# Last layer of a three-layer model: GpSimd makes half of the low weight halves, the convolution sums in PSUM, heads read their queries in place

## The reference, cut to what matters

```
h    = rms_norm(stream)                       # 272 x 1024
proj = h @ w_in                               # conv input 2048, q 1024, k 256, v 256, q_idx 512, k_idx 64, w_idx 8, gates 2048
q, k, q_idx, k_idx = rope(...)                # rotary embedding: x*cos + rotate(x)*sin
a, gate = split(u_conv); c = a * sigmoid(gate)
c = sum over w in 0..30 of c[t-30+w] * dw_w[w]  + dw_b      # 31 taps per channel, 1024 channels
y_a = silu(layer_norm(c)) @ pw_out
score = sum over 8 index heads of w_idx * relu(q_idx . k_idx / 8)     # which keys a query may see
keep the 68 best keys of each query (meta keys always)
y_b = softmax(q . k, kept keys only) . v  @ w_o               # 8 heads of 128, 2 key groups
stream += (sigmoid(g_a) * y_a + sigmoid(g_b) * y_b) @ w_merge
stream += ffn(...); out = rms_norm(stream)
```

## Time and profile before

| what | us |
|---|---|
| median of the runs shown | 1202.35 |
| the profiled execution's own time | 1201.14 |
| its span | 1199.4 |
| TensorE busy | 1140.1 (95%) |
| VectorE busy | 793.7 (66%) |
| ScalarE busy | 573.8 (48%) |
| GpSimd busy | 81.7 (7%) |

### The profile page before, as it was taken

How to read it: one execution, slowest core, us unless ns; L and a number is a source line. 1 busy time by engine, 2 the same in 40 slices (tenths; PEclk the granted TensorE clock), 3 DMA queues, 4 the chain that set the end, 5 groups by cost and what they waited for, 6 DMA issues and landing times.

```text
span 1199.4 us, 22503 instructions
## 1 busy us (share of the span) xinstructions
PE 1140.1 (95%) x8981; PEld 1097.4 (91%) x8981; DVE 793.7 (66%) x1260; ACT 573.8 (48%) x818; POOL 81.7 (7%) x85
## 2 busy tenths in 40 slices
PE   5998899999999999999999899898899998999998
PEld 4997799999999999999999799798678998999997
DVE  4546755555557776565555598999878666778743
ACT  4546744444445565444444533342456536565541
POOL 0003020000113110200000000100100000000000
PEclk9999899999999999999999999999898998999999
DMA  7662064654775333565456364343221553545360
GB/s 222 208 195 71 4 208 141 198 178 159 228 254 175 127 122 106 181 206 181 152 191 204 110 172 154 120 138 112 69 71 55 164 169 109 198 151 191 124 211 36
DMA packets 190773, 181.74 MB, mean 152 GB/s; under 512 B 20911, under 2 KB 189116, under 8 KB 190699
## 3 DMA queue, kind: packets, MB, share of 16 engines
q1 hardware_dynamic: 190171, 178.61, 47.1%
q0 software_dynamic: 528, 2.10, 0.6%
HBM read 179.64 MB, written 1.05 MB: 151 GB/s over the span
## 4 chain that ended last, share of the span: by engine, by line
PE 84%; DVE 9%; ACT 4%; issue 1%; DMA 1%; POOL 1%; SPq 1%; DVEq 0%; ACTq 0%; POOLq 0%
PE ps L495 25%; PE ps L496 24%; PE ps L497 24%; DVE work L2088 3%; PE ps L651 2%; DVE w_lo L356 2%; PE ps L804 1%; ACT w_hi L347 1%; PE ps L908 1%; DMA conv_rows<-in_conv_dw_w 1%; POOL work L421 1%; PE ps L642 1%; PE ps L404 1%; PE ps L1687 1%; PE ps L1850 1%
## 5 line engine op out<-in xcount | busy, mean ns | idle before, releaser
L495 PE MATMUL ps<-u_hi,w_hi 128*128 128x256 f32 (+2 forms) x1864 | 534.3, 287 | 17.1 <-DVE u_lo L464 8.7
L496 PE MATMUL ps<-u_lo,w_hi 128*128 128x256 f32 (+2 forms) x1864 | 530.3, 284 | 0.0
L497 PE MATMUL ps<-u_hi,w_lo 128*128 128x256 f32 (+2 forms) x1864 | 529.6, 284 | 0.0
L356 DVE TENSOR_TENSOR w_lo<-raw,w_hi 128x2048 fp32r<-128x2048 f32 (+5 forms) x184 | 386.0, 2107 | 173.2 <-ACT w_hi L347 172.7
L495 PEld LDWEIGHTS ps<-u_hi,w_hi 128*128 128x128 f32 x1864 | 356.2, 191 | 20.1 <-issue 17.1
L497 PEld LDWEIGHTS ps<-u_hi,w_lo 128*128 128x128 f32 x1864 | 356.1, 191 | 0.0
L496 PEld LDWEIGHTS ps<-u_lo,w_hi 128*128 128x128 f32 x1864 | 355.7, 191 | 0.5
L347 ACT ACTIVATE w_hi<-raw 128x2048 fp32r<-128x2048 f32 (+5 forms) x184 | 319.6, 1755 | 29.7 <-PE ps L497 29.5
L496 PE MATMUL ps<-a_lo,w_hi 128*128 128x256 f32 x528 | 148.0, 280 | 0.0
L497 PE MATMUL ps<-a_hi,w_lo 128*128 128x256 f32 x528 | 147.6, 280 | 0.0
L495 PE MATMUL ps<-a_hi,w_hi 128*128 128x256 f32 x528 | 147.0, 278 | 0.1
(11 more groups left out here) (285 smaller groups left out, 1294.4 us busy)
## 6 DMA issues: line engine op xcount, KB each, us to landing
raw<-in_w_in SPq DMA_DIRECT2D x24, 1024.0 KB, 5.3
raw<-in_w_gate SPq DMA_DIRECT2D x22, 1024.0 KB, 5.4
raw<-in_w_up SPq DMA_DIRECT2D x22, 1024.0 KB, 5.4
raw<-in_ffn_up SPq DMA_DIRECT2D x22, 1024.0 KB, 5.1
raw<-in_w_down SPq DMA_DIRECT2D x16, 768.0 KB, 4.8
raw<-in_od_w_qkv SPq DMA_DIRECT2D x12, 1024.0 KB, 5.2
raw<-in_w_down SPq DMA_DIRECT2D x16, 640.0 KB, 4.6
raw<-in_ev_w_in SPq DMA_DIRECT2D x8, 1024.0 KB, 8.3
```

Of the source, the lines that this page charges most:

```text
L356: nc.vector.tensor_tensor(w_lo[t % RING][:, 0:n], raw[t % RAW][:, 0:n], w_hi[t % RING][:, 0:n].bitcast(F32), ALU.subtract).then_inc(lo_don ...
L495: nc.tensor.matmul(out_ap, a_h, b_h, start=start and n == 0, stop=False)
L496: nc.tensor.matmul(out_ap, a_h, b_l, start=False, stop=False)
L497: mm = nc.tensor.matmul(out_ap, a_l, b_h, start=False, stop=stop and n == len(pairs) - 1)
```

## The change

VectorE no longer makes the low halves of units 3, 5, 7, ... 21; GpSimd does, in four pieces of 128x512 each, with a semaphore of its own (`pool_lo_done`), for which TensorE and SyncE then wait. The convolution's sums of the first three pairs of tiles lie in PSUM banks 6 and 7 and are written to `work` with the last tap; those of the fourth pair stay in SBUF. Rope and index scores are moved to banks 4 and 5 alone. The steps of the convolution are dealt out anew: 30 in `ph_conv`, 14 in `ph_idx`, 18 in `ph_proj`, 1 and 12 as before, then 15 in one loop behind `ph_gate` (all that is left of the first three pairs), then the fourth pair's 30 between the attention heads. The index heads multiply the queries in place by two zero-padded copies of the keys (`ki_half`, made by ScalarE), the attention heads read `q_d` in place, and GpSimd's sixteen copies of queries go.

```
@@ -251,7 +251,7 @@
         k_d = sb("k_d", [P, KVH, T2], scope=s)
         v_d = sb("v_d", [P, 3, KVH * DH], scope=s)
         wi = sb("wi", [P, 3, IH], scope=s)
-        q_cur = sb("q_cur", [P, 2, T2], scope=s)
+        ki_half = sb("ki_half", [P, 2, T2], scope=s)
         pick = sb("pick", [P, 416], BF16, scope=s)
         top8 = sb("top8", [P, 2, 8], scope=s)
         need = sb("need", [P, 2], scope=s)
@@ -318,8 +318,11 @@
             count[(ph.u0 + n) % RAW] += 16 * d
             landed.append(count[(ph.u0 + n) % RAW])
 
+    pool_units = [ph_conv.u0 + n for n in range(3, 23, 2)]
+
     raw_landed = [sem(f"raw_landed{n}") for n in range(RAW)]
     hi_done, lo_done, unit_done = sem("hi_done"), sem("lo_done"), sem("unit_done")
+    pool_lo_done = sem("pool_lo_done")
     pair_read = [sem(f"pair_read{n}") for n in range(4)]
 
     def pairs_read(eng, ph):
@@ -346,11 +349,31 @@
         wait(nc.scalar, unit_done, turn * ph.body + (t - (RING - 1)))
         nc.scalar.activation(w_hi[t % RING][:, 0:n], raw[t % RAW][:, 0:n], ACT.Copy).then_inc(hi_done, 1)
 
+    def wait_lo(eng, u, first=0):
+
+        if isinstance(u, int):
+            if u in pool_units:
+                eng.wait_ge(pool_lo_done, pool_units.index(u) + 1)
+                return
+            first = u
+        wait(eng, lo_done, u + (1 - sum(t < first for t in pool_units)))
+
+    def split_lo_pool(t):
+
+        nc.gpsimd.wait_ge(hi_done, t + 1)
+        for piece in range(4):
+            cols = slice(piece * UNIT // 4, (piece + 1) * UNIT // 4)
+            a = nc.gpsimd.tensor_tensor(w_lo[t % RING][:, cols], raw[t % RAW][:, cols], w_hi[t % RING][:, cols].bitcast(F32),
+                                        ALU.subtract)
+        a.then_inc(pool_lo_done, 1)
+
     def split_lo(ph, i, k):
 
         if (u := split_unit(ph, i, k)) is None:
             return
         turn, t, n = u
+        if t in pool_units:
+            return
 
         nc.vector.wait_ge(hi_done, turn * ph.body + (t + 1))
         nc.vector.tensor_tensor(w_lo[t % RING][:, 0:n], raw[t % RAW][:, 0:n], w_hi[t % RING][:, 0:n].bitcast(F32),
@@ -512,7 +535,7 @@
     def begin_unit(ph, i, k):
         s = (ph.u0 + k) % RING
 
-        nc.tensor.wait_ge(lo_done, ph.unit(i, k) + 1)
+        wait_lo(nc.tensor, ph.unit(i, k), ph.u0)
         if k % ph.group == 0:
 
             wait(nc.tensor, pair_read[ph.pair(k)], ph.used_before(i, k))
@@ -1093,7 +1116,8 @@
 
     def begin_load(ph, i, k):
 
-        wait(nc.sync, lo_done, ph.unit(i, k) - (RAW - 1))
+        if not isinstance(i, int) or ph.unit(i, k) >= RAW:
+            wait_lo(nc.sync, ph.unit(i, k) - RAW, ph.u0)
         nc.sync.sem_inc(sem("slot_taken"), 1)
         s = (ph.u0 + k) % RAW
         return raw[s], raw_landed[s]
@@ -1263,24 +1287,11 @@
         fold_squares("final", T1)
 
         pairs_read(pool, ph_down1)
-        for n, t in enumerate((cin[:, :, 0:CONV_W - 1], stat4[:], q_cur[:])):
+        for n, t in enumerate((cin[:, :, 0:CONV_W - 1], stat4[:], ki_half[:])):
             nc.gpsimd.memset(t, 0.0).then_inc(sem("zeroed"), 1)
             pool.wait_ge(sem("zeroed"), 4 + n)
-        pool.wait_ge(sem("rope_done"), 8)
-        for n in range(IH):
-            e = n % 2
-            rows = slice(64 * e, 64 * e + 64)
-            wait(pool, sem("idx_pad"), n)
-            wait(pool, sem("idx_scored"), n - 1)
-            nc.gpsimd.tensor_copy(q_cur[rows, e, :], qi[rows, n // 2, :]).then_inc(sem("idx_pad"), 1)
-        pool.wait_ge(sem("idx_scored"), IH)
-        pool.wait_ge(sem("idx_pad"), IH)
-        pool.wait_ge(sem("rope_done"), 18)
-        for i, e in dsa.steps(pool):
-            n = dsa.head(i, e)
-            wait(pool, sem("at_scores"), n + (dsa.base - 1))
-            wait(pool, sem("pad_done"), n + dsa.base)
-            nc.gpsimd.tensor_copy(q_cur[:, e % 2, :], q_d[:, n, :]).then_inc(sem("pad_done"), 1)
+        for t in pool_units:
+            split_lo_pool(t)
         fold_squares("ffn2", NF)
         fold_squares("final2", T1)
 
@@ -1510,12 +1521,19 @@
                 nc.scalar.activation(v_d[0:META, 0, :], ps[0:META, 2 * p, UC:2 * UC], ACT.Copy)
                 a = nc.scalar.activation(v_d[:, 1:3, :], pair_ap(p, UC), ACT.Copy)
             a.then_inc(pair_read[p], 1)
+            if k == 1:
+
+                act.wait_ge(sem("rope_done"), 8)
+                act.wait_ge(sem("zeroed"), 6)
+                for e in range(2):
+                    rows = slice(64 * e, 64 * e + 64)
+                    nc.scalar.activation(ki_half[rows, e, :], ki[rows, :], ACT.Copy).then_inc(sem("idx_pad"), 1)
             if k == 2:
 
                 for n in range(IH):
                     act.wait_ge(sem("idx_scored"), n + 1)
                     wait(act, sem("idx_acc"), n - 1)
-                    nc.scalar.activation(dots(n % 2), ps[:, 6 + n % 2, 0:416], ACT.Relu, scale=ID ** -0.5)\
+                    nc.scalar.activation(dots(n % 2), ps[:, 4 + n % 2, 0:416], ACT.Relu, scale=ID ** -0.5)\
                         .then_inc(sem("idx_relu"), 1)
         for i, k in ph_gate.steps(act):
             split_hi(ph_gate, i, k)
@@ -1821,15 +1839,16 @@
             if k == 0:
                 pairs_read(pe, ph_idx)
                 pairs_read(pe, ph_conv)
-                rope_pe(c("rot64"), idx_tiles, T2, 3, [4, 5, 6, 7])
+                rope_pe(c("rot64"), idx_tiles, T2, 3, [4, 5])
             if k == 2:
                 pe.wait_ge(sem("rope_done"), 8)
+                pe.wait_ge(sem("idx_pad"), 2)
                 for n in range(IH):
                     e = n % 2
-                    pe.wait_ge(sem("idx_pad"), n + 1)
                     wait(pe, sem("idx_relu"), n - 1)
-                    nc.tensor.matmul(ps[:, 6 + e, 0:144], q_cur[:, e, META:META + P], ki[:, 0:144], start=True, stop=True)
-                    nc.tensor.matmul(ps[:, 6 + e, 144:416], q_cur[:, e, META + P:T2], ki[:], start=True, stop=True)\
+                    qh, kh = qi[:, n // 2, :], ki_half[:, e, :]
+                    nc.tensor.matmul(ps[:, 4 + e, 0:144], qh[:, META:META + P], kh[:, 0:144], start=True, stop=True)
+                    nc.tensor.matmul(ps[:, 4 + e, 144:416], qh[:, META + P:T2], kh, start=True, stop=True)\
                         .then_inc(sem("idx_scored"), 1)
         uh_f, ul_f = (lambda kt: u_hi[:, kt, CF]), (lambda kt: u_lo[:, kt, CF])
         for i, k in ph_gate.steps(pe):
@@ -1838,16 +1857,16 @@
                 pairs_read(pe, ph_proj)
                 pe.wait_ge(sem("idx_relu"), IH)
                 lo, hi = Q_ROPES[k]
-                rope_pe(c("rot128"), q_tiles[lo:hi], T2, 8 + lo, [4, 5, 6, 7])
+                rope_pe(c("rot128"), q_tiles[lo:hi], T2, 8 + lo, [4, 5])
         pairs_read(pe, ph_gate)
         pe.wait_ge(sem("rope_done"), 18)
         pe.wait_ge(sem("pick_ready"), 1)
+        pe.wait_ge(sem("conv_tap"), 2 * (KT // 2 - 1) * (CONV_W - 1))
 
         def dsa_scores(att, i, e, n):
-            pe.wait_ge(sem("pad_done"), n + (att.base + 1))
             for b, (q0, nq, keys) in enumerate(att.blocks):
                 end = keys[-1][0] + keys[-1][1]
-                nc.tensor.matmul(att.S(e, b), q_cur[:, e % 2, q0:q0 + nq], k_d[:, i, 0:end], start=True, stop=False)
+                nc.tensor.matmul(att.S(e, b), q_d[:, n, q0:q0 + nq], k_d[:, i, 0:end], start=True, stop=False)
                 mask = seen_b[0:META, 0:META] if b == 0 else pick[:, 0:144] if b == 1 else pick[:, 144:416]
                 mm = nc.tensor.matmul(att.S(e, b), ident_b[0:nq, 0:nq], mask, start=False, stop=True)
             return mm
@@ -2085,13 +2104,19 @@
                     src, tap = cin[:, tile, w + CF.start:w + CF.stop], conv_w[:, tile, w:w + 1]
                     if w > 1:
                         dve.wait_ge(sem("conv_tap"), (j * (CONV_W - 1) + w - 1) * 2 + tile % 2 - 1)
-                    nc.vector.scalar_tensor_tensor(out=work[:, tile, 0:NF], in0=src, scalar=tap, in1=work[:, tile, 0:NF],
-                                                   op0=ALU.mult, op1=ALU.add).then_inc(sem("conv_tap"), 1)
+                    elif j:
+                        dve.wait_ge(sem("conv_tap"), j * (CONV_W - 1) * 2 + tile % 2 - 1)
+                    kept, summed = work[:, tile, 0:NF], ps[:, 6 + tile % 2, 0:NF]
+                    if j == KT // 2 - 1:
+                        summed = kept
+                    nc.vector.scalar_tensor_tensor(out=kept if w == CONV_W - 1 else summed, in0=src, scalar=tap,
+                                                   in1=kept if w == 1 else summed, op0=ALU.mult, op1=ALU.add)\
+                        .then_inc(sem("conv_tap"), 1)
 
         for i, k in ph_conv.steps(dve):
             split_lo(ph_conv, i, k)
             if k >= 2:
-                conv(5 if k in (4, 6) else 4)
+                conv(4 if k % 2 == 0 else 6)
             if k % 2:
                 p, gate = ph_conv.pair(k), ph_conv.pair(k - 1)
                 dve.wait_ge(unit_done, ph_conv.unit(i, k) + 1)
@@ -2100,7 +2125,7 @@
```

(10 more changed lines are left out.)

35 lines of the change are left out of this document (21 added, 14 removed).

## The result

The changed kernel takes 1225.19 us (median of four runs, 1223.75 to 1225.8); the kernel before, run beside it, 1202.02. The ratio is 1.0194, with a 95% interval of 1.0178 to 1.021: 23.2 us slower. The profiled execution of after has a span of 1223.4 us against 1199.4.

The account below looks back on a forecast made before the run. The bound was the TensorE-VectorE chain to the mask (`pick`). Block 12.3 us, two-bank ropes, holds and clock start the attention 19.4 later; with -0.45 behind, +19.0 on 1201.14 gives 1220.1 profiled, 1221.3 median; range 1215 to 1228.

Parts of the forecast that it names:

- The case that got 0.54: Chain to the mask: bare block and two-bank ropes both lengthen it; 1215 to 1228 us, chance 0.54.
- The block: Between the split of unit 23 and the mask: 30 tap instructions at 0.409 us, 12.3 us bare on the chain.
- my own sign: Ahead of the mask: the prediction is wrong if the block takes other than 12 to 14.5 us.
- Rope in two banks: Rope groups: third and fourth products wait for adds, 0.84 us a round trip, 0.65 more a tile; index group +3.4.
- a lowered clock: TensorE at unit 19: matmuls at 1.2 GHz for a while instead of 2.4, 1.25 us added.
- Holds by GpSimd: Second rope group, instructions reading two SBUF tiles, during GpSimd's split of unit 21: 0 to 4 us, 2.0 taken.
- GpSimd as a cover: GpSimd's low halves: 4.6 to 5.2 us a unit, 7.5 at worst, with no wait of TensorE.
- Index heads: No pause; first acc at 774.85 against 774.55, the gain there paying for the rope; GpSimd's copies were hidden.
- Behind the attention: After the attention: 13 steps go, but unit and sums hide them, so only -0.45 us.
- A: Rival, chain to unit 20: ropes cost nothing, only the block stays; 1206 to 1215 us, chance 0.22.
- B: Rival, VectorE's total work decides as TensorE never holds it up: faster, 1199.8 us, chance 0.07.
- C: Rival, units 13 to 21: GpSimd also holds single-SBUF-input instructions, up to 1.2 us a piece; 1228 to 1245, chance 0.13.

Follow-up runs that it names:

- e1_fill: The changed kernel with the block of 15 steps dealt out into three of VectorE's waits; 1213.26 us, 1.0092 of the kernel before.
- e4_in_place: The kernel before with only the heads reading their queries in place and GpSimd's 16 copies gone; 1200.95 us, 0.9992 of before.
- e3_two_banks: The kernel before with only rope put in two PSUM banks instead of four; 1217.73 us, 1.013 of before.
- e9_spread_fill2: The changed kernel with rope dealt out at most two tiles behind a unit and the block's 15 steps placed elsewhere; 1193.11 us, 0.9935 of before.

## Why the prediction was right, point by point

- **Direction and size.** Forecast +19.0, measured +23.2. The case that got 0.54, block and ropes together, is what happened. For the profiled execution I had 1220.1 and it took 1225.17. Of these 5.1 us some 1.65 lay ahead of the change, where two executions differ. The ropes and the holds made 3.3 up to unit 20, and 0.45 I had expected to gain behind the attention. The block gave 0.5 back.
- **The block.** 12.3 forecast, 11.8 in the trace, 11.9 by e1_fill. By my own sign this was a miss, if a narrow one: I had called the prediction wrong if the block took other than 12 to 14.5 us. The slip is in the price of a tap. My 0.409 was the length of a row of 8, which holds the tail of the last one; from start to start the SBUF taps of before come every 0.399 us (8 from 752.16 to 755.35), and those of the block every 0.394. Nothing is to be seen of a higher price for PSUM: with the sum in PSUM a tap takes 481 ns (median of 168), and with it in SBUF 481 ns (of 60).
- **Rope in two banks** is the term that was mis-sized. The mechanism was right: TensorE idle before every third and fourth product (758.58 to 762.50 after), unit 19 behind the second add of its group. Up to the end of unit 20 I had 7.2 us, the trace has 10.5 (845.43 is just inside the 846 that I had set as a limit). Half of what is missing, 1.6 us, lies in the index group and unit 12, and 1.4 between the heads and the second add of the second q group, where the low-clock round trips and the holds below fall together. I took 0.84 us for every round trip, but at the low clock the product alone takes 1.27, and VectorE's idle spell is 1.37 and not 0.82 us. Behind the index group unit 12 ran partly at 1.2 GHz: from its start near 763.8 to its copy at 770.76, 7.0 us instead of 5.97. I had granted a lowered clock to unit 19 alone. How much this costs differs between executions: in e1_fill, the same kernel up to there, the low clock comes one product earlier (1.22 us at 761.06), and the copy of unit 12 comes 15.6 us behind that of unit 11, against 14.5.
- **Holds by GpSimd.** I allowed 2.0 us in one rope group, and only for instructions with two SBUF inputs. There were three places on the chain: 1.45 instead of 0.56 at the index heads' first instructions, which read one SBUF tile, 1.45 instead of 0.43 in the first rope group, 1.13 and 0.58 instead of 0.44 in the second; together 2.7 us.
- **GpSimd as a cover.** 5.0 to 5.3 us for most units, 7.1 for the first, whose pieces met a split: inside my 4.6 to 7.5, and no wait of TensorE for any of them.
- **Index heads.** With a pause of 0.42 us where before had 2.70, nearly as forecast, and VectorE now waits for the first score (4.26 us). That GpSimd's copies of queries were hidden is not quite right: they held VectorE's taps by 1.0 us ahead of the heads (e4_in_place), though the time doesn't show it.
- **Behind the attention.** I forecast -0.45; the span from its start shows 0.0. This rest took 352 to 358 us in the eleven profiled executions of the changed kernel and the experiments, so no such gain can be told there.
- **The rivals.** A (ropes free) falls by e3_two_banks. B, faster because VectorE sheds more than it takes on, did not happen here, but it is what e9_spread_fill2 does once ropes and block are out of the way. C falls for the taps by the 5.06 and 7.96 us rows beside PSUM sums, and came true in one place, for 0.9 us at the index heads. The prediction's sentence on a single SBUF input leaves out the exception that the Trainium skill makes in that section, for the modes that use both ports.

## What to carry to other kernels

Work that is moved off an engine pays only if what comes next on the chain is no longer than what went: here a helper engine took 22 us of splits, and 12 us of taps in the wrong place with a halved ring of banks cost 24 to 28. Here a group of four or five products through two banks made the two engines wait for each other product by product; deal such a group out so that it never exceeds the banks. Keep the sums that VectorE carries along in PSUM while GpSimd works beside it: here that was worth 10.8 us. And place filler work where the trace shows its engine idle, not behind the last instruction whose input comes late.

## What the runs showed of the hardware that I had not expected

In the changed kernel TensorE went from 2.4 to 1.2 GHz (the granted clock is 0.50 from 763 to 765) in the course of three idle spells of 1.2 to 1.5 us each, with single products between them. The index heads before, with one spell of 2.70 us, kept the full clock:

```profile
775.86 0.48 PE L1831 MATMUL ps<-ki,q_cur 128*128 128x144 f32 x2 [2.70 <-ACT sg L1518]
```
```profile
774.00:776.00 2.00, 0.14 (x1) 0.17 (x2) 1.89 (x6) 0.52 (x1) 0.00 (x0) 1.00 0.72 255
```

The spells alone don't settle it. In the second q group of e3_two_banks, spells of 2.38 and 1.24 us left both products at 0.72 us; in the changed kernel, with 2.69 and 1.92, the second took 1.28. And e1_fill had the same spells as the changed kernel within 0.01 us, with the low clock one product earlier. A loop between two engines then also pays in its own round trips: 1.96 us from product to product at the high clock (758.58 to 760.54), 2.50 at the low one (813.97 to 816.47).
